# RMS norm roots kept as one number per token on the partitions and spread over the channels by TensorE

## What is computed

```python
def rms_norm(x, g):
    xf = x.astype(jnp.float32)
    y = xf * lax.rsqrt(jnp.mean(xf * xf, axis=-1, keepdims=True) + EPS)
    return (y * g.astype(jnp.float32)).astype(x.dtype)

def modulate(x, g, shift, scale):
    return rms_norm(x, g) * (1.0 + scale) + shift

def ffn_sublayer(x, shift, scale, gate, g_pre, g_post, wg, wu, wd):
    y = swiglu(modulate(x, g_pre, shift, scale), wg, wu, wd)
    return x + FFN_RES * gate * rms_norm(y, g_post)
```

## Time and profile before

| | |
|---|---|
| median of 3 runs | 2300.18 us (2296.97 to 2301.59) |
| the profiled execution | 2304.52 us, its span 2302.4 us |
| PE busy | 2045.6 us, 89% of the span |
| DVE busy | 908.9 us, 39% |
| ACT busy | 777.4 us, 34% |
| mean granted PE clock | 0.911 of full speed |

### The profile page before, as it was taken

How to read it: one execution, slowest core, us unless ns; L and a number is a source line. 1 busy time by engine, 2 the same in 40 slices (tenths; PEclk the granted TensorE clock), 3 DMA queues, 4 the chain that set the end, 5 groups by cost and what they waited for, 6 DMA issues and landing times.

```text
span 2302.4 us, 25421 instructions
## 1 busy us (share of the span) xinstructions
PE 2045.6 (89%) x10581; PEld 1600.3 (70%) x10581; DVE 908.9 (39%) x1287; ACT 777.4 (34%) x1130; POOL 194.9 (8%) x287
## 2 busy tenths in 40 slices
PE   5999999979975767999999989999997995869997
PEld 2777778838843555677777858888783873658997
DVE  1433232264454354432332263333226445355544
ACT  3422222245234222422222243222224534235443
POOL 3011110025100000111110010000002400000000
PEclk8999999989987558999999989999998997579998
DMA  7455543343200012455553343333234430044653
GB/s 260 128 176 164 173 152 96 91 122 74 74 19 1 0 37 76 144 166 164 173 152 118 97 120 106 95 92 93 78 89 116 111 86 1 0 128 128 184 161 114
DMA packets 363778, 250.86 MB, mean 109 GB/s; under 512 B 30242, under 2 KB 341876, under 8 KB 363664
## 3 DMA queue, kind: packets, MB, share of 16 engines
q1 hardware_dynamic: 343024, 179.80, 28.5%
q0 software_dynamic: 20640, 69.44, 9.3%
HBM read 248.15 MB, written 1.05 MB: 108 GB/s over the span
## 4 chain that ended last, share of the span: by engine, by line
PE 79%; DVE 8%; ACT 7%; issue 2%; DMA 2%; SPq 1%; POOLq 0%; POOL 0%; DVEq 0%; ACTq 0%
PE bank L303 22%; PE bank L304 21%; PE bank L305 21%; PE bank L1345 3%; PE bank L1666 2%; ACT tmp_b L579 2%; PE bank L1376 1%; PE bank L1369 1%; PE bank L1648 1%; PE bank L1574 1%; DVE rstd L851 1%; ACT u_hi L583 1%; DVE w_lo L287 1%; ACT w_hi L279 1%; PE bank L1523 1%
## 5 line engine op out<-in xcount | busy, mean ns | idle before, releaser
L303 PE MATMUL bank<-u_hi,w_hi 128*128 128x512 f32 (+2 forms) x1872 | 695.2, 371 | 43.7 <-DVE u_lo L868 18.2
L304 PE MATMUL bank<-u_lo,w_hi 128*128 128x512 f32 (+2 forms) x1872 | 683.7, 365 | 0.0
L305 PE MATMUL bank<-u_hi,w_lo 128*128 128x512 f32 (+2 forms) x1872 | 683.2, 365 | 0.0
L287 DVE TENSOR_TENSOR w_lo<-raw,w_hi 128x2048 fp32r<-128x2048 f32 (+2 forms) x182 | 373.9, 2054 | 362.7 <-ACT w_hi L279 362.4
L303 PEld LDWEIGHTS bank<-u_hi,w_hi 128*128 128x128 f32 (+1 forms) x1872 | 358.1, 191 | 148.0 <-issue 55.7
L305 PEld LDWEIGHTS bank<-u_hi,w_lo 128*128 128x128 f32 (+1 forms) x1872 | 358.1, 191 | 57.9 <-issue 1.4
L304 PEld LDWEIGHTS bank<-u_lo,w_hi 128*128 128x128 f32 (+1 forms) x1872 | 358.9, 192 | 51.5
L279 ACT ACTIVATE w_hi<-raw 128x2048 fp32r<-128x2048 f32 (+2 forms) x182 | 311.5, 1711 | 165.7 <-PE bank L305 145.3
L303 PE MATMUL bank<-ht_hi,w_hi 128*128 128x512 f32 (+1 forms) x704 | 257.4, 366 | 9.9 <-DVE ht_lo L894 8.2
L304 PE MATMUL bank<-ht_lo,w_hi 128*128 128x512 f32 (+1 forms) x704 | 256.6, 364 | 0.0
L305 PE MATMUL bank<-ht_hi,w_lo 128*128 128x512 f32 (+1 forms) x704 | 256.5, 364 | 0.0
(11 more groups left out here) (234 smaller groups left out, 1612.0 us busy)
## 6 DMA issues: line engine op xcount, KB each, us to landing
ada_slot<-in_ada_w_dram POOLq DMA_DIRECT2D x128, 512.0 KB, 4.4
raw<-in_ffn_wg_dram SPq DMA_DIRECT2D x88, 512.0 KB, 4.0
raw<-in_ffn_wu_dram SPq DMA_DIRECT2D x88, 512.0 KB, 5.2
raw<-in_ffn_wd_dram SPq DMA_DIRECT2D x64, 384.0 KB, 3.6
raw<-in_ffn_wd_dram SPq DMA_DIRECT2D x64, 320.0 KB, 4.1
raw<-in_w_in_dram SPq DMA_DIRECT2D x32, 512.0 KB, 5.1
ada_first<-in_ada_w_dram SPq DMA_DIRECT2D x4, 2048.0 KB, 20.7
raw<-in_w_in_dram SPq DMA_DIRECT2D x16, 256.0 KB, 4.7
```

The costliest lines, as they stand in the source:

```text
L287: nc.vector.tensor_tensor(w_lo[s][:, 0:size], raw[s][:, 0:size], w_hi[s][:, 0:size].bitcast(F32), ALU.subtract).then_inc(lo_ready[s], 1)
L303: nc.tensor.matmul(acc, wh, xh, start=first, stop=False)
L304: nc.tensor.matmul(acc, wh, xl, start=False, stop=False)
L305: return nc.tensor.matmul(acc, wl, xh, start=False, stop=last)
```

## The change

The sums of squares are put with the tokens on the partitions. Of each 128 tokens the squares become the stationary operand and one column of ones the moving one, so that the sum is one column of a PSUM bank; four columns hold 512 tokens. Root and reciprocal then work on a 128x4 tile (128x2 for 256 tokens), `root_in` or `root_out`. A new step `spread` on PE multiplies each column, repeated 128 times as the stationary operand, with the identity: this puts the number of each token on all 128 partitions, in bank 5 for the norm ahead and bank 7 for the norm behind. DVE's sixteen multiplications read that bank in place of `rstd`.

```diff
-        rstd = own("rstd", [P, TOK])
+        root_in = own("root_in", [P, TT])
+        root_out = own("root_out", [P, TT])
...
-            def mean_root(T, need, ready, need_count):
+            def mean_root(T, root, sums, need, ready, need_count):
...
-                nc.scalar.activation(rstd[:, 0:T], bank[7][:, 0:T], ACT.Sqrt, bias=eps_col[:], scale=1.0 / DM)\
+                nc.scalar.activation(root[:, 0:T // P], sums[:, 0:T // P], ACT.Sqrt, bias=eps_col[:], scale=1.0 / DM)\
                     .then_inc(ready, 1)
...
-            def invert(need, need_count, ready, ready_count, T):
-                dve.wait_ge(need, need_count)
-                nc.vector.reciprocal(rstd[:, 0:T], rstd[:, 0:T]).then_inc(ready, 1)
-                dve.wait_ge(ready, ready_count)
+            def invert(root, need, ready, count, T):
+
+                dve.wait_ge(need, count)
+                nc.vector.reciprocal(root[:, 0:T // P], root[:, 0:T // P]).then_inc(ready, 1)
...
                 dve.wait_ge(mod_done, MODS_BEFORE[z])
+                dve.wait_ge(norm["rstd_spread"], z + 1)
...
-                    nc.vector.tensor_tensor(tmp_b[k % 2][:, 0:T], H[:, k, 0:T], rstd[:, 0:T], ALU.mult)\
+                    nc.vector.tensor_tensor(tmp_b[k % 2][:, 0:T], H[:, k, 0:T], bank[5][:, 0:T], ALU.mult)\
...
                 dve.wait_ge(mod_done, MODS_BEFORE_POST[z])
+                dve.wait_ge(post["ss_spread"], z + 1)
...
-                    nc.vector.tensor_tensor(tmp_b[k % 2][:, 0:T], Y[:, k, 0:T], rstd[:, 0:T], ALU.mult)\
+                    nc.vector.tensor_tensor(tmp_b[k % 2][:, 0:T], Y[:, k, 0:T], bank[7][:, 0:T], ALU.mult)\
...
+            def spread(root, to, T, ready, count, done):
+
+                pe.wait_ge(ready, count)
+                for tt in range(T // P):
+                    last = nc.tensor.matmul(to[:, tt * P:(tt + 1) * P], root[:, tt:tt + 1].to_broadcast([P, P]), ident[:],
+                                            start=True, stop=True)
+                last.then_inc(done, 1)
+
             def norm_in(z, T):
                 for k in range(KT):
                     pe.wait_ge(norm["sq_ready"], KT * z + k + 1)
-                    nc.tensor.matmul(bank[7][:, 0:T], ones[:], tmp_a[k % 2][:, 0:T], start=(k == 0), stop=(k == KT - 1))\
-                        .then_inc(norm["sq_used"], 1)
+                    for tt in range(T // P):
+                        last = nc.tensor.matmul(bank[5][:, tt:tt + 1], tmp_a[k % 2][:, tt * P:(tt + 1) * P], ones[:, 0:1],
+                                                start=(k + tt == 0), stop=(k == KT - 1 and tt == T // P - 1))
+                    last.then_inc(norm["sq_used"], 1)
...
                     ada_quarters(o, (2, 3))
-                    turn_block(o)
+                spread(root_in, bank[5], T, norm["rstd_ready"], z + 1, norm["rstd_spread"])
+                if z - 1 in TURN:
+                    turn_block(TURN[z - 1][0] + 1)
...
                 pe.wait_ge(post["ysq_added"], KT * z + KT)
-                nc.tensor.matmul(bank[7][:, 0:T], ones[:], sq_sum[:, 0:T], start=True, stop=True).then_inc(post["ss_done"], 1)
+                for tt in range(T // P):
+                    last = nc.tensor.matmul(bank[7][:, tt:tt + 1], sq_sum[:, tt * P:(tt + 1) * P], ones[:, 0:1], start=True, stop=True)
+                last.then_inc(post["ss_done"], 1)
                 if z in TURN:
                     ada_quarters(TURN[z][0], (2, 3))
+                spread(root_out, bank[7], T, post["ss_rstd"], z + 1, post["ss_spread"])
```

More of the change, by code:

```diff
@@ L240, in hybrid_block_kernel @@
                              "out_turned", "out_copied", "out_stored", "mix_cleared", "mix_loaded"))
-        NORM = ("sq_ready", "sq_used", "rms_ready", "rstd_ready", "scaled", "moded", "uhi_ready", "u_ready")
+        NORM = ("sq_ready", "sq_used", "rms_ready", "rstd_ready", "rstd_spread", "scaled", "moded", "uhi_ready", "u_ready")
         GATED = ("silu_ready", "prod_ready", "hthi_ready", "ht_ready")
-        POST = ("y_ready", "ysq_ready", "ysq_added", "ss_done", "ss_rms", "ss_rstd", "y_scaled", "h_added")
+        POST = ("y_ready", "ysq_ready", "ysq_added", "ss_done", "ss_rms", "ss_rstd", "ss_spread", "y_scaled", "h_added")
         MIX = ("proj_ready", "tile_done", "v_turned", "v_ready", "vm_ready", "rot_done", "rope_step", "score", "max_step",
@@ L567, in norm_in @@
                     nc.scalar.activation(tmp_a[k % 2][:, 0:T], H[:, k, 0:T], ACT.Square).then_inc(norm["sq_ready"], 1)
-                mean_root(T, norm["sq_used"], norm["rms_ready"], KT * z + KT)
+                mean_root(T, root_in, bank[5], norm["sq_used"], norm["rms_ready"], KT * z + KT)
                 if z == 0:
@@ L620, in down @@
                 steps(act, KT // 2, body)
-                mean_root(T, post["ss_done"], post["ss_rms"], z + 1)
+                mean_root(T, root_out, bank[7], post["ss_done"], post["ss_rms"], z + 1)
             def project(layer, m, T):
@@ L857, in norm_in @@
                     modulation(TURN[z - 1][0])
-                invert(norm["rms_ready"], z + 1, norm["rstd_ready"], z + 1, T)
+                invert(root_in, norm["rms_ready"], norm["rstd_ready"], z + 1, T)
                 if z == 0:
@@ L909, in post_norm @@
             def post_norm(layer, q, z, T, Y):
-                invert(post["ss_rms"], z + 1, post["ss_rstd"], z + 1, T)
+                invert(root_out, post["ss_rms"], post["ss_rstd"], z + 1, T)
                 dve.wait_ge(mod_done, MODS_BEFORE_POST[z])
+                dve.wait_ge(post["ss_spread"], z + 1)
                 def scale(k):
                     wait(dve, post["h_added"], KT * z + k - 1)
-                    nc.vector.tensor_tensor(tmp_b[k % 2][:, 0:T], Y[:, k, 0:T], rstd[:, 0:T], ALU.mult)\
+                    nc.vector.tensor_tensor(tmp_b[k % 2][:, 0:T], Y[:, k, 0:T], bank[7][:, 0:T], ALU.mult)\
                         .then_inc(post["y_scaled"], 1)
```

## The result

The changed kernel takes 2353.4 us in the median of 4 runs (2349.1 to 2362.19), the kernel before 2300.88 us beside it. The ratio is 1.0237 (95% interval 1.0205 to 1.0269): slower by 52 us, where +16 was forecast. The spans of the profiled executions are 2350.3 and 2302.4 us, so 47.9 us are to be found in the traces.

What follows compares the result with a forecast made beforehand. Mostly PE products (79% of the chain), untouched; the change touches turns between sublayers, where PE starves. Terms 12.0 + 3.2 + 2.0 - 1.0 = +16.2 us on 2304.52, or 2316.4 from the median 2300.18; range 2309 to 2325.

Steps and rivals of the forecast that it cites:

- the place of spread in the norms behind: Turns 0 to 3: on PE spread follows ada_w quarters 2 and 3, so DVE waits for their transfers; +12.0 us.
- I take 14.6: Turns 0 to 3: time in us from DVE's first multiplication behind to the root ahead, from measured 15.47 and 14.44.
- turn 4: Passage from sublayer z = 4 to the next, with 256 tokens: +2.0 us, between +1.2 and +2.6.
- the sums cost as much as before; I put nothing for them: Eight one-column PE instructions per sum: 1.05 us at full clock, 1.87 at half, against the old sum's 1.12.
- the norms ahead: Turns 0 to 3: last quarter and spread make root to multiplication 4.7 to 5.4 us, not 4.11; +0.8 each, +3.2.
- signs that I named, the last: Profile sign for a right forecast: the last root stands about 3 us later after each turn's start.
- more clock lost: Rival, chance 0.12: PE idles around spread, clock stays at 1.2 GHz through the sums; +26 us, about 2326.
- 2 us a turn: In the clock rival: further loss of each turn if the pace is beyond 15.47 us.
- The remark against it: Against the clock rival: PE is busy longer in one piece, 3.7 + 1.9 us, which may raise the clock sooner.
- The last norm: Norm behind the last sublayer (z = 5), no quarter in the way: shorter root and reciprocal, plus spread; -1.0 us.
- nothing for the source in PSUM: DVE's multiplications by rstd now read PSUM: no added time put, though the skill page gives 0.065 us per instruction.
- Faster: Rival, chance 0.06: quarters are through before the reciprocal, so spread does not wait in effect; -15 us, about 2285.

Runs made afterwards that it cites:

- both, sums of 128 columns: Changed kernel with sums of 128 columns of ones in place of one and both spreads ahead of quarters 2 and 3: 2295.27 us, ratio 0.9977.

## Why the prediction was wrong

**Right: the place of spread in the norms behind.** Forecast were multiplications at 474.0, or 9.15 us after the sum in turn 0; measured 9.01, and 16.01, 9.67, 8.37 in turns 1 to 3 (forecast 15.8, 8.6, and 8.3). `spread` took 2.08 us at half clock where 1.9 was put and 1.16 at full where 1.2 was put. The run of the norms behind with the spread moved ahead shows that this place is worth about 20 us.

**Wrong: "I take 14.6", the time from the first multiplication to the root ahead.** It measured 22.04, 22.24, 22.23 and 22.23 us. Four times 7.6 us are 30 of the 36 us that the forecast missed; turn 4 adds most of the rest (+7.5 where +2.0 was put). There the cause is mostly the same: its squares were sums of one column too, and from its first square to the root it takes 13.1 us, against 9.0 before and 9.6 with sums of 128 columns. The step behind it was the sentence "the sums cost as much as before; I put nothing for them". The two rows it rested on were right: a group takes 1.05 us at full clock and 1.87 at half. What I left out is that these rows are at a clock which other work had set. With the old sums of 512 columns in this place the clock came to 1.00 (14.6 and 16.1 us to the root in the run of the norms behind only); with sums of one column in the same place, and nothing changed between the sum behind and the squares, it stayed at 0.50 (22.2 us in turns 0 and 2 in the run of the norms ahead only). I carried over the pace of the turns before, which contained the rise to 1.00, to sums that do not bring it. Of the signs that I named, the last failed: the root of turns 0 to 3 stands 10.3 to 11.4 us later, not about 3.

**The rival "more clock lost" named the right thing, the granted clock, and the wrong reason.** It looked for the loss in PE idling. The trace shows the reverse: PE is busy for 14.0 of 14.0 us between 480 and 494 at 0.50. PE's idle 2.90 us ahead of the first sum may have a part in the fall near 476, but in the run of the norms ahead only no `spread` is waited for there and the clock is at 0.50 all the same. Its 2 us a turn, put beyond the slowest pace seen before without a row for them, became 7.5. The remark against it, that a longer busy piece would bring the clock up sooner, came true and did not help: the clock is at 0.92 on the mean of 472 to 475, where the kernel before is at 0.50 until 476, and it fell again under the sums. The Trainium skill, "TensorE: Matmul & The Clock Gate", Part 1, says that activity releases the clock; by that it should have risen within this stretch. The trace does not agree, if activity is read as the profile's busy column.

**Right in size, in part by luck: the norms ahead.** From the root to the multiplication it takes 4.96, 4.92, 4.64 and 4.38 us in place of 4.11; +0.8 was put for each. But the path was another. Forecast was a wait for the last quarter's transfer and then work at full clock. In turn 0 both quarters run back to back from 494.15 for 2.97 us with no wait, at a granted clock of 0.50, and `spread` takes 2.08: the last load was issued 3.2 us ahead of the root in place of 1.6, as the sums between took longer, and the slow clock took the gain back. The forecast's own path is seen with sums of 128 columns: in turn 0 PE waits 1.41 us for the last transfer, `spread` takes 1.16, and it is 4.58 us from the root to the multiplication. The last norm takes 2.12 us from its sum to the multiplication in place of 3.10: -1.0, as put.

**Right: nothing for the source in PSUM.** Groups by shape on DVE, after, for the earlier trace rows:

```profile
L875 DVE TENSOR_TENSOR tmp_b<-H,bank 128x512 f32<-128x512 f32 x40 | 27.0, 686 | 18.1 <-PE bank L1380 17.0
...
L919 DVE TENSOR_TENSOR tmp_b<-Y_ffn,bank 128x512 f32<-128x512 f32 x24 | 16.2, 686 | 23.0 <-PE bank L1380 22.4
```

The group of the kernel before that answers to the first, with both sources in SBUF:

```profile
L873 DVE TENSOR_TENSOR tmp_b<-H,rstd 128x512 f32<-128x512 f32 x40 | 27.2, 691 | 1.2
```

686 ns with `bank` as a source, against 691 with `rstd` and 691 for the group of the earlier trace rows; the pair of the earlier trace rows takes 1.29 us in both kernels. The 62 cycles more that the Trainium skill, "VectorE: DVE Perf Modes", has for such a source do not show.

**Rivals.** "Faster" was the case in which `spread` does not wait. The runs made that case by order, and it came out at -3.5 us (norms behind only) and -7.4 us (both, sums of 128 columns), not -15. Moving ACT's row copies brought it to -14.8; that this meets the rival's -15 is a coincidence, since the rival left the copies where they were.

## What to carry to other kernels

When a change makes matmuls narrow, do not take over the duration that the same shape has elsewhere in the trace: look at the granted clock of that row, and ask whether the clock will be the same where the new matmuls stand, once the wide ones are gone. Here a moving operand of 128 columns in place of one gave 29 us back. And before a result is routed through an engine that the consumer did not need, read what stands ahead of it in that engine's order: a wait for a transfer there becomes the consumer's wait, and moving one call up, ahead of the quarters, was worth 20 us where the clock was not hurt.

## What the hardware showed that was not expected

- PE wholly busy (14.0 of 14.0 us, 480 to 494, weight loads in 12.2 of them) at a granted clock of 0.50, that is 1.2 GHz, in the changed kernel; with sums of 128 columns it was at 1.00 from 480 to 494.
- The same one-column group took 1.87 us at half clock and 0.95 us at full, between matmuls of 512 columns.
- DVE multiplied 128x512 in 686 ns with one source in PSUM and 691 ns with both in SBUF.
